# Gather rows turned back by TensorE, and six adaLN chunks loaded beside a query selection

## The reference, cut to what matters

```python
for i in range(DEPTH):                                    # DEPTH = 2
    mod = (c_act @ ada_w[i] + ada_b[i])[:, None, :]
    sh1, sc1, g1, sh2, sc2, g2 = jnp.split(mod, ADA_CHUNKS, axis=-1)
    h = _rmsnorm(x, norm_mix_g[i]) * (1.0 + sc1) + sh1
    m = conv(h) if i == 0 else attention(h)
    x = x + g1 * m
    h = _rmsnorm(x, norm_ffn_g[i]) * (1.0 + sc2) + sh2    # the modulated rows
    x = x + g2 * _peer(h, pk_w_q[i], pk_keys[i], pk_u[i], pk_v[i])
return _rmsnorm(x, final_g)
```

## Time and profile before

| | us |
|---|---|
| median of three runs | 3162.95 |
| lowest and highest | 3157.99, 3164.09 |
| the profiled execution, its own time | 3159.37 |
| its span | 3157.8 |

### The profile page before, as it was taken

How to read it: one execution, slowest core, us unless ns; L and a number is a source line. 1 busy time by engine, 2 the same in 40 slices (tenths; PEclk the granted TensorE clock), 3 DMA queues, 4 the chain that set the end, 5 groups by cost and what they waited for, 6 DMA issues and landing times. The chain is left out here.

```text
span 3157.8 us, 45163 instructions
## 1 busy us (share of the span) xinstructions
PE 2909.9 (92%) x12846; PEld 2091.0 (66%) x12846; DVE 2340.9 (74%) x4896; ACT 536.2 (17%) x1358; POOL 1514.1 (48%) x1566
## 2 busy tenths in 40 slices
PE   6998988999999999999899988769999999999997
PEld 4776756777666665555587867657667776655554
DVE  3999799887888867666532664998888888667676
ACT  2123215200000000000233152143000000000001
POOL 0001355455555577676200261553555555777774
PEclk8998988999999999999999999889999999999999
DMA  7544354699999999999633322235999999999998
GB/s 314 229 173 162 124 208 160 245 410 402 410 409 404 407 410 410 410 410 410 261 141 120 122 79 80 107 113 192 410 409 408 401 407 405 410 410 410 410 409 316
DMA packets 242919, 957.20 MB, mean 303 GB/s; under 512 B 26969, under 2 KB 27145, under 8 KB 225162
## 3 DMA queue, kind: packets, MB, share of 16 engines
q0 software_dynamic: 147456, 536.94, 43.1%
q1 hardware_dynamic: 95370, 419.17, 34.4%
HBM read 953.90 MB, written 2.10 MB: 303 GB/s over the span
## 5 line engine op out<-in xcount | busy, mean ns | idle before, releaser
L908 PE MATMUL out_e<-weights,mod_rows 128*128 128x512 f32 x2048 | 933.3, 598 | 60.9 <-DVE mod_rows L1644 59.3
L899 PE MATMUL acc<-h_t,weights 128*128 128x256 f32 x4096 | 930.3, 380 | 0.0
L899 PEld LDWEIGHTS acc<-h_t,weights 128*128 128x128 f32 x4096 | 780.8, 191 | 218.8 <-issue 125.1
L495 POOL DMA_INDIRECT v_rows<-in_pk_v,idx_now x512 | 635.6, 1241 | 573.3 <-DVE mod_rows L1582 457.8
L1582 DVE SCALAR_TENSOR_TENSOR mod_rows<-v_rows,acts,mod_rows 128x1024 f32<-128x1024 f32 x512 | 657.6, 1284 | 201.2 <-DMA v_rows<-in_pk_v,idx_now 198.0
L908 PEld LDWEIGHTS out_e<-weights,mod_rows 128*128 128x128 f32 x2048 | 376.3, 190 | 469.4 <-issue 368.3
L1565 DVE SCALAR_TENSOR_TENSOR u_rows<-u_rows,h_rows 128x1024 f32<-128x1024 f32 x512 | 625.5, 1222 | 80.5 <-DMA u_rows<-in_pk_u,idx_now 79.4
L489 POOL DMA_INDIRECT u_rows<-in_pk_u,idx_now x512 | 570.4, 1114 | 235.2 <-issue 144.2
L521 POOL CAST top_f<-top_i 128x64 f32<-128x64 uint32 x32 | 7.6, 238 | 747.4 <-DVEq L1523 736.6
L1255 ACT ACTIVATE mod_rows<-acc 128x256 f32<-128x256 f32 x256 | 98.1, 384 | 1199.0 <-PE acc L899 1195.5
L1644 DVE TENSOR_TENSOR mod_rows<-mod_rows,region 128x256 f32<-128x256 f32 x256 | 109.6, 428 | 184.9 <-ACT mod_rows L1255 182.4
(11 more groups left out here) (241 smaller groups left out, 2426.6 us busy)
## 6 DMA issues: line engine op xcount, KB each, us to landing
weights<-in_u_t SPq DMA_DIRECT2D x256, 512.0 KB, 6.7
weights<-in_pk_v SPq DMA_DIRECT2D x256, 512.0 KB, 6.8
weights<-in_pk SPq DMA_DIRECT2D x32, 1024.0 KB, 4.8
v_rows<-in_ada SPq DMA_DIRECT2D x30, 1024.0 KB, 6.7
weights<-in_w_qkv SPq DMA_DIRECT2D x24, 1024.0 KB, 4.8
weights<-in_w_in SPq DMA_DIRECT2D x16, 1024.0 KB, 7.7
weights<-in_ada SPq DMA_DIRECT2D x14, 1024.0 KB, 4.9
weights<-in_w_out SPq DMA_DIRECT2D x8, 1024.0 KB, 4.8
```

The costliest lines, as they stand in the source:

```text
L495: nc.gpsimd.indirect_dma_start(v_rows[:, r % VR, :], None, a["pk_v"], bass.IndirectOffsetOnAxis(ap=idx_now[:, 1, par, r:r + 1], axis=0)).t ...
L899: last = nc.tensor.matmul(acc[s][:, 0:HALF], weights[:, s, k * P:(k + 1) * P], h_t[:, k, :], start=k == 0, stop=k == KB - 1)
L908: last = nc.tensor.matmul(out_e[2 * tt + c][:, :], e_act[:, s, tt * P:(tt + 1) * P], weights[:, s, D + c * 512:D + (c + 1) * 512], start=F ...
```

## The change

`gather_rows`, `scale_row`, the two loads of `g_ffn_row` and the rows `sh2_row` and `sc2_row` go. PE turns the modulated columns of the second half back into rows (`back`, eight transposes for each 128 tokens, into banks `out_e[2]` and `out_e[3]`), after heads 2 and 4 of `select(l, 1)`; ACT copies them into `h_rows` (`take_back`, two copies each). `spread_rows` makes four halves instead of eight. In `peer` PE, not ACT, waits for both rows. Of the twelve late chunks six are now loaded into six slots of `region`, one behind each of the first six query loads of layer 0's second half; PE multiplies these six, then the six that remain late.

```diff
-LATE = 12
+LATE, SPARES = 6, 6
...
+        spare_slots = [region[:, at:at + CHUNK] for at in (0, 2048, 4336, 6384, 12800, 14848)]
...
-                    sp.dma_start(g_ffn_row, a["g_ffn"][0, :].partition_broadcast(P)).then_inc(g_ffn_in, 16)
...
+                if at[:3] == ("pk", 0, 1) and at[3] < SPARES:
+
+                    sp.dma_start(spare_slots[at[3]], a["ada1"][ADA_CHUNKS - LATE - SPARES + at[3], :, :]).then_inc(spare_in[at[3]], 16)
...
-                if at == ("qkv", 1, 0, QKV[1]):
-
-                    sp.wait_ge(e_act_ready, NK)
-                    sp.dma_start(g_ffn_row, a["g_ffn"][1, :].partition_broadcast(P)).then_inc(g_ffn_in, 16)
...
-                        row = (G1, SH2, SC2, G2)[i // 2] + i % 2 * 2 + c
+                        row = (G1, G2)[i // 2] + i % 2 * 2 + c
...
+            def back(l, tt):
+
+                pe.wait_ge(h_t_ready, norm_no(l, 1, 1, tt) + 1)
+                if tt:
+                    pe.wait_ge(h_rows_ready, 2 * l + 1)
+                for k in range(KB):
+                    last = nc.tensor.transpose(out_e[2 + k // 4][:, k % 4 * P:(k % 4 + 1) * P],
+                                               columns_of[1][:, k, tt * P:(tt + 1) * P], ident[:, :])
+                last.then_inc(back_full, 1)
...
-                pe.wait_ge(rows_done, DEPTH)
+                pe.wait_ge(rows_ready, 4 * DEPTH)
...
+                pe.wait_ge(h_rows_ready, 2 * l + 2)
...
-                    spread_rows(0, (2 * i - 8, 2 * i - 7), [out_e[3], mid[0]])
+                    spread_rows(0, (i - 4,), [out_e[3], mid[0]])
...
-            select(0, 1)
+            select(0, 1, between={2: lambda: back(0, 0), 4: lambda: back(0, 1)})
             score(0, 1, PH - 1)
+            for n in range(SPARES):
+                pe.wait_ge(spare_in[n], 16)
+                ada_chunk(ADA_CHUNKS - LATE - SPARES + n, spare_slots[n], out_e[0], False)
...
-            norm(1, 1, 0, lambda: spread_rows(1, range(4), out_e))
+            norm(1, 1, 0, lambda: spread_rows(1, range(2), out_e))
...
-            norm(1, 0, 0, lambda: spread_rows(1, range(4, 8), out_e))
+            norm(1, 0, 0, lambda: spread_rows(1, range(2, 4), out_e))
...
+            def take_back(l, tt):
+                act.wait_ge(back_full, 2 * l + tt + 1)
+                for c in range(2):
+                    last = nc.scalar.activation(h_rows[:, tt, c * 512:(c + 1) * 512], out_e[2 + c][:, :], ACT.Copy)
+                last.then_inc(h_rows_ready, 1)
...
-                act.wait_ge(h_rows_ready, 2 * l + 2)
...
-            select(0, 1)
+            select(0, 1, between={2: lambda: take_back(0, 0), 4: lambda: take_back(0, 1)})
...
-            select(1, 1, between={3: lambda: exps(1, 0)})
+            select(1, 1, between={2: lambda: take_back(1, 0), 3: lambda: exps(1, 0), 4: lambda: take_back(1, 1)})
...
-            scale_row(0)
...
-                if head == 2:
-                    for tt in range(2):
-                        gather_rows(0, tt)
```

More of the change, by code:

```diff
@@ L165, in build @@
         mod_rows = sb("mod_rows", [P, 3 * D])
-        g1_row, sh2_row, sc2_row = (mod_rows[:, i * D:(i + 1) * D] for i in range(3))
+        g1_row = mod_rows[:, 0:D]
         g2_row = sb("g2_row", [P, D])
@@ L251, in build @@
         c_sq = region[:, 12800:14848].rearrange("p (k t) -> p k t", k=KB)
-        g_ffn_row = region[:, 15360:16384]
         final_row = region[:, 0:1024]
@@ L282, in col @@
             return cols[:, at:at + size] if i is None else cols[:, i + at:i + at + n]
-        cols_in, b_out_in, g_ffn_in, final_in, keys_in = map(sem, ("cols_in", "b_out_in", "g_ffn_in", "final_in", "keys_in"))
+        cols_in, b_out_in, final_in, keys_in = map(sem, ("cols_in", "b_out_in", "final_in", "keys_in"))
         x_in = [sem(f"x_in{h}") for h in range(2)]
@@ L293, in build @@
         late_used = sem("late_used")
+        spare_in = [sem(f"spare_in{i}") for i in range(SPARES)]
         acc_full, acc_free, ada_used = sem("acc_full"), sem("acc_free"), sem("ada_used")
-        c_silu_ready, c_pad_ready, strips_ready, ada_full, ada_ready, cols_full, rows_full, mod_ready, rows_ready, rows_done = map(
+        c_silu_ready, c_pad_ready, strips_ready, ada_full, ada_ready, cols_full, rows_full, mod_ready, rows_ready, back_full = map(
             sem, ("c_silu_ready", "c_pad_ready", "strips_ready", "ada_full", "ada_ready", "cols_full", "rows_full", "mod_ready",
-                  "rows_ready", "rows_done"))
+                  "rows_ready", "back_full"))
         root_ready, rstd_ready, xn_ready, xn_t_full, h_t_ready, h_rows_ready = map(
@@ L668, in spread_rows @@
                     if i >= len(banks):
-                        pe.wait_ge(rows_ready, 8 * l + i - len(banks) + 1)
+                        pe.wait_ge(rows_ready, 4 * l + i - len(banks) + 1)
                     for c in range(2):
-                        row = (G1, SH2, SC2, G2)[i // 2] + i % 2 * 2 + c
+                        row = (G1, G2)[i // 2] + i % 2 * 2 + c
                         last = nc.tensor.matmul(banks[i % len(banks)][:, c * NC:(c + 1) * NC],
@@ L1007, in _ @@
             score(1, 0, PH - 1)
-            select(1, 1)
+            select(1, 1, between={2: lambda: back(1, 0), 4: lambda: back(1, 1)})
             score(1, 1, PH - 1)
@@ L1061, in spread_rows @@
             def spread_rows(l, halves, banks):
-                rows = [g1_row, sh2_row, sc2_row, g2_row]
+                rows = [g1_row, g2_row]
                 for i in halves:
-                    act.wait_ge(rows_full, 8 * l + i + 1)
+                    act.wait_ge(rows_full, 4 * l + i + 1)
                     nc.scalar.activation(rows[i // 2][:, i % 2 * 512:(i % 2 + 1) * 512], banks[i % len(banks)][:, :], ACT.Copy
@@ L1312, in _ @@
             squares(1, 0, 0)
-            spread_rows(1, range(4), out_e)
+            spread_rows(1, range(2), out_e)
             norm(1, 0, 0)
             take(1, 0, 1)
-            spread_rows(1, range(4, 8), out_e)
+            spread_rows(1, range(2, 4), out_e)
             take(1, 0, 2)
@@ L1740, in _ @@
             reciprocal_root(1, 0, 0)
-            scale_row(1)
             attention(0)
@@ L1759, in _ @@
                 rank(1, 1, head)
-                if head == 2:
-                    for tt in range(2):
-                        gather_rows(1, tt)
                 if head == 5:
@@ L1797 @@
         "w_qkv": chunked(a["sb_w_qkv"][0]), "w_o": chunked(a["sb_w_o"][0]),
-        "b_out": a["cv_b_out"][0], "g_ffn": a["norm_ffn_g"], "final_g": a["final_g"], "ada_b": a["ada_b"],
+        "b_out": a["cv_b_out"][0], "final_g": a["final_g"], "ada_b": a["ada_b"],
         "pk_u": a["pk_u"].reshape(DEPTH * NK * NK, D), "pk_v": a["pk_v"].reshape(DEPTH * NK * NK, D),
```

9 lines of the change are left out of this document (removed).

## The result

| us | before | after |
|---|---|---|
| median, five runs each on one chip | 3164.09 | 3148.01 |
| lowest and highest | 3157.99, 3166.75 | 3143.87, 3152.48 |
| the profiled execution, its own time | 3159.37 | 3152.48 |
| its span | 3157.8 | 3150.7 |

The ratio is 0.9948, with a 95% interval of 0.9937 to 0.996: 16 us less, between 13 and 20. The forecast was 3145, with a range of 3139 to 3154. The profiled execution of after is the slowest of its five, so the two spans differ by 7 us only.

A forecast was written before the change was run, and what follows sets the result against it. The long loops, at the DMA limit, stay untouched; only the last-ending waits before them and at the layer boundary count. Terms 8.6 + 2.0 + 6.6 = 17.2 us gave 3145 us, range 3139 to 3154.

The forecast's parts named there:

- clock rival: Layer 0's first gates: TensorE's clock falls after idling; gain 5.4 us there, 14.0 in all, about 3149 us; chance 0.23.
- a sign that was named against the forecast: In DVE's ranking: new idle time ahead of its first maxima would show the forecast wrong.
- The gather rows, 6.6 us a layer: Second-half selection, both layers: removing four DVE operations per layer counts in full, 6.6 us each.
- unbroken: Second-half selection: DVE ranks without a pause, so the removed gather rows' 6.6 us a layer count in full.
- lower price of 4.9 us a layer: Gather rows priced at a dot's 1.22 us each, if lost time moves to other DVE work; whole gain 3.5 less.
- What takes their place, 0: Second-half selection: PE's added transposes and ACT's copies cost 0; 0 to 2.2 us per layer if cover failed.
- The six chunks: Layer 0's second-half selection: six chunks loaded early let PE finish clears and first block at 481.7, 13 us earlier.
- What is late next in layer 0, 8.6 us: Layer 0, one-hots to first dot: dot at 494.2 against 502.80, gain 8.6 us, bounds 7.7 and 9.7.
- The boundary, 2.0 us: Between the layers: halving the row spread frees PE earlier, ACT then ends last; gain 2.0 us.
- Bounds 1.0 to 2.8: Layer boundary: limits set on the forecast gain of 2.0 us from spreading two halves instead of four.
- Drowned: Second-half selection: added PE blocks or slowed weight loads make scores late; some 2 us gain left, about 3161; chance 0.08.
- slower: Long expert loops: a poorer starting distance between row gathers and table loads lengthens them; 3174 us; chance 0.04.

The follow-up runs named there:

- warm_both: warm_edge with eight more idle-time matmuls ahead of the first gates of each layer; 3143.37 us, ratio 0.9949.
- chunks_only: The kernel before, gather rows kept on DVE, with six late chunks loaded beside the selection; 3164.62 us, ratio 0.9992.
- after_again: The kernel after, unchanged, run and profiled once more; 3150.5 us, ratio 0.9945.
- warm_edge: The kernel after with eight idle-time matmuls before the layer boundary's first transposes and five ahead of the projection; 3141.86 us, again 3142.19.

## Why the prediction held, point by point

The number held, its three terms less so: 7.2 to 7.5 us came for 8.6, nothing for 2.0, and 5.4 to 5.9 for 6.6. The mechanism was right where DVE is relieved, and wrong where TensorE's clock comes in. That 16 us came of it and not less is in part luck: by stages the three profiles gave 12.4 us in the mean, below even the clock rival's 14.0, and 3.2 us of the runs' gain are in no stage that the change touches. Of the forecast's signs, DVE did wait for PE, PE idled 5.6 us and not 3, the boundary didn't shrink by 2 us, and in layer 1 DVE's idle time ahead of the second list's maxima grew (2.05 us for 1.18), which comes near to a sign that was named against the forecast.

**The gather rows, 6.6 us a layer: right.** In layer 0 the stretch from the first maxima to the one-hots fell from 118.62 to 111.84 us, 6.8. In layer 1 from 94.71 to 88.91, 5.8; 0.9 of the difference is the wait at the second list, 2.05 us in place of 1.18 (against the first maxima DVE is there 0.3 us earlier, and the list comes 0.6 later). PE's work up to that list is the same in both, 13.98 us of projections without a pause and then the scores; it is DVE's first maxima that come 0.6 us earlier against it. This one list is bound by PE in both kernels, so in layer 1 "unbroken" was wrong. The lower price of 4.9 us a layer, for operations slowed by the look-up that would have moved their lost time elsewhere, falls: the rows as measured were the better guide. That GpSimd is slowed at the same place shows only now. The prediction's 5.19 us stood beside no other row. POOL's timeline before, the look-up ahead of that one, and that of after at the place of the 5.19 us:

```profile
413.15 2.60 POOL L529 TENSOR_TENSOR u_rows<-u_rows 128x512 f32<-128x512 f32 x3
```

```profile
425.22 2.61 POOL L530 TENSOR_TENSOR u_rows<-u_rows 128x512 f32<-128x512 f32 x3
```

**What takes their place, 0: right.** Each block of eight transposes took 1.04 us, the second list's wait stands ahead of the first block in layer 1, and the third list, the tightest, had no wait.

**The six chunks: right**, with PE ready 2.5 us sooner than forecast, and the experiments show that this half of the change is what lets the other count in layer 0.

**What is late next in layer 0, 8.6 us: mis-sized, 7.2 to 7.5 in three profiles.** Of the 8.6 us, 1.9 stood behind the first one-hots, and 0.5 to 0.7 of these came: from there to the loop it took 84.7 and 84.6 us in the two profiles before, and 84.2, 84.0 and 83.9 in the three of after. Two steps failed. One is "the third starts there if PE's first gates take the 1.95 us": they took 3.48 to 3.78, after 5.6 to 5.9 us of idle time instead of 3.3, PE having been too early by those 2.5 us. The other is that the first dot's gain was taken for the loop's. In the first profile the dot did come as forecast, 13.1 us behind the one-hots, but the gates behind it were slow too, and from dot to loop it took 71.0 us, not 69.7; in the other two the dot came 14.2 to 14.3 behind, and the loop 69.7 after it. `warm_both` bears this out: with first gates of 2.05 us its loop came no more than 0.5 us sooner. The rival "TensorE's clock falls again" was right in its mechanism and too dear in its price, 5.4 for layer 0. Whether the turned picks have a part in it, as the rule cited there would have it, no run shows.

**The boundary, 2.0 us: the step "Bounds 1.0 to 2.8" was wrong.** The projection did start 1.96 us earlier (1.69 and 1.95 in the other two profiles), and the same projection took 1.7 to 2.9 us longer, so the stage gave 0.3, 0.0 and -0.9 us. The bounds held the time that was removed on PE, and priced the projection behind it at one clock level only, though it stands behind 2.56 us without work. Nor is half of 5.56 us right for half of the spread: the sixteen were at the half clock only in part (3.62 us at the full one), and the eight took 2.6 to 3.6 us. What made the projection slow in after and not in the two profiles before stays open, since `chunks_only` has it slow with the old boundary.

**Layer 1, 6.6 us: 5.4 to 5.9**, for the wait at the second list, and up to 0.5 us behind the one-hots.

**Sum.** 17.2 forecast; 10.8, 14.0 and 12.5 by stages of the three profiles; 13.9 to 16.9 by runs. The 1.4 to 5.3 us between stages and runs stay open. For `after` a good part is the profiled execution, 4.5 us above its median; in the other two the sum by stages lies within the interval of the ratio, and the start varies by more. "Drowned" and "slower" fall: no wait for weights at the lists, and long loops that go by the chip. (One loop of `after_again` is 4.1 us longer than that of the earlier trace rows, beyond the 3 us that were to speak against the forecast, but one of `chunks_only` on that chip, the gather rows still on DVE, is as long: 980.01 against 977.25 and 976.44.)

**The best version.** `warm_edge` was 17.4 and 17.6 us below the kernel before. On the third chip it was 3.8 us below the kernel after (3142.19 against 3145.97, five runs each, whose ranges overlap), which its stages bear out (17.1 against 12.5).

## What to carry to other kernels

When two engines meet at one place and each is late by a little, taking work off one alone moves the wait, and the gain shows only once the other gets as much: read how long the waiting engine could still run ahead before you price either part. A gain of 2 us on TensorE's path can be lost in the matmuls behind the next short wait, which may run at either clock level: price such a stage at both. One or two profiles don't tell which level it will be; look at every profile of the same code, the ones made for other questions too. If the idle time can't be removed, a few matmuls of no use inside it, right ahead of the work on the path, held the clock here in every profile, while the same ones elsewhere gave nothing or cost time.

## What the runs showed of the hardware

- The same 32 matmuls behind the same 2.56 us without work took 7.17, 8.86, 9.67, 10.07 or 10.20 us. With the same code ahead they took 7.17 or 8.86 (a spread of sixteen, at 5.56 and 4.79 us), and 8.86 or 10.07 (a spread of eight). With 0.39 us without work it was 7.17 three times.
- Transposes follow the clock: eight took 1.97 us behind 5.03 us of idleness, and 1.09 to 1.10 behind other matmuls at the full clock.
- Three additions of 128x512 on GpSimd took 5.19 us beside DVE's gather rows and 2.61 at the same place without them; DVE's own gather rows took 1.36 to 2.18 us, a dot of their shape 1.22.
- Two chips gave the long loops 976 us, and a third 978 to 981 us at 399 in place of 401 GB/s, in every kernel tried on it.
